# A fused two-block kernel: one more buffer for the experts' weights, and four pieces of side work moved

## What is computed

```
for i in (0, 1):                                   # first block
    mix = gla_mixer(h) if i == 0 else mlstm_mixer(h)
    h = layer_norm(ALPHA * h + mix)
    h = layer_norm(ALPHA * h + grouped_moe(h))     # 16 experts, 2 per token
for l in (0, 1):                                   # second block
    parts = split((rms(x) * (1 + sc1) + sh1) @ w_in[l])
    y_a, y_b = gqa_attention(rope(q), rope(k), v), dilated_attention(...)
    x = x + gt1 * ((gate_a * y_a + gate_b * y_b) @ w_out[l])
    x = x + gt2 * (square(relu(h2 @ w_ff1[l])) @ w_ff2[l])

def grouped_moe(x):
    for e in range(16):
        h = silu(t @ w1[e]) * (t @ w3[e])
        y = y + gates[:, e:e + 1] * (h @ w2[e])
```

## Time and profile before

| what | value |
| --- | --- |
| median of 3 runs | 1483.88 us (1482.96 to 1484.76) |
| profiled execution, its own time | 1485.66 us |
| its span, first to last instruction | 1483.8 us |
| PE busy | 1443.6 us, 97% |
| DVE, ACT, POOL busy | 910.2, 626.7, 40.8 us |
| mean granted TensorE clock | 0.993 |
| moved by DMA | 420.17 MB, mean 283 GB/s |

### The profile page before, as it was taken

The page is one execution under the profiler, slowest core; times in us unless marked ns, Lnnn a source line. Parts: engine busy times, 40 slices in busy tenths (PEclk is TensorE's granted clock), DMA queues, the critical chain, the costliest instruction groups (busy, mean ns, idle before and its releaser), DMA issues.

```text
span 1483.8 us, 20474 instructions
## 1 busy us (share of the span) xinstructions
PE 1443.6 (97%) x8383; PEld 1068.5 (72%) x8383; DVE 910.2 (61%) x1549; ACT 626.7 (42%) x1004; POOL 40.8 (3%) x39
## 2 busy tenths in 40 slices
PE   9999999989999999999799999999999999999998
PEld 7885444436888544443578897999988898799997
DVE  4986111118787611111799888997968976775555
ACT  6453211115334321211555655454456566465443
POOL 0000000000000000000210000000002000000000
PEclk9999999999999999999899999999999999999999
DMA  9897999998467899999665463899955533445540
GB/s 379 314 365 301 426 427 426 427 426 329 166 247 297 331 424 427 427 426 426 247 231 184 181 232 142 335 369 352 357 182 187 197 123 125 151 170 193 179 168 29
DMA packets 59062, 420.17 MB, mean 283 GB/s; under 512 B 6657, under 2 KB 6721, under 8 KB 8658
## 3 DMA queue, kind: packets, MB, share of 16 engines
q1 hardware_dynamic: 58322, 417.17, 71.5%
q0 software_dynamic: 640, 1.61, 0.4%
HBM read 417.71 MB, written 1.05 MB: 282 GB/s over the span
## 4 chain that ended last, share of the span: by engine, by line
PE 80%; DVE 11%; DMA 4%; ACT 3%; issue 1%; SPq 0%; DVEq 0%; ACTq 0%
PE ps L869 78%; DVE lo L2111 2%; DMA AR<-in_moe 2%; DMA raw<-in_moe 2%; DVE AR L2104 2%; PE ps L1520 1%; DMA AR<-in_wgu 1%; DVE AR L2101 1%; PE ps L1491 1%; ACT AR L2011 1%; PE ps L1244 1%; DVE TINY L2104 1%; DVE ACC L2104 0%; PE ps L991 0%; PE ps L1001 0%
## 5 line engine op out<-in xcount | busy, mean ns | idle before, releaser
L2111 DVE TENSOR_TENSOR lo<-raw,hi 128x1024 fp32r<-128x1024 f32 x296 | 359.4, 1237 | 97.7 <-ACT hi L1661 97.0
L1661 ACT ACTIVATE hi<-raw 128x1024 fp32r<-128x1024 f32 x296 | 306.2, 1056 | 183.3 <-PE ps L869 178.1
L869 PE MATMUL ps<-T,hi 128*128 128x256 f32 x1792 | 323.8, 283 | 1.4 <-DVE lo L2111 0.6
L869 PE MATMUL ps<-hi,T 128*128 128x512 f32 x896 | 285.8, 396 | 1.0 <-DVE lo L2111 0.6
L869 PEld LDWEIGHTS ps<-T,hi 128*128 128x128 f32 x1792 | 277.1, 189 | 10.0 <-issue 5.1
L869 PE MATMUL ps<-T,lo 128*128 128x256 f32 x896 | 249.2, 280 | 0.0
L869 PEld LDWEIGHTS ps<-hi,T 128*128 128x128 f32 x896 | 169.0, 189 | 38.0 <-DVE lo L2111 2.1
L869 PE MATMUL ps<-lo,T 128*128 128x512 f32 x448 | 172.8, 390 | 0.0
L869 PEld LDWEIGHTS ps<-T,lo 128*128 128x128 f32 x896 | 169.2, 189 | 0.3 <-DVE lo L2111 0.3
L869 PE MATMUL ps<-hi,AF 128*128 128x512 f32 x512 | 163.3, 391 | 0.0
L2104 DVE SCALAR_TENSOR_TENSOR AR<-AR,ps 128x512 f32<-128x512 f32 x52 | 35.4, 684 | 192.0 <-PE ps L869 104.8
(11 more groups left out here) (247 smaller groups left out, 1730.5 us busy)
## 6 DMA issues: line engine op xcount, KB each, us to landing
raw<-in_moe SPq DMA_DIRECT2D x76, 1024.0 KB, 17.1
raw<-in_b_ff SPq DMA_DIRECT2D x64, 1024.0 KB, 5.3
AR<-in_moe SPq DMA_DIRECT2D x59, 1024.0 KB, 17.1
raw<-in_ada SPq DMA_DIRECT2D x48, 1024.0 KB, 6.7
ring<-in_moe SPq DMA_DIRECT2D x45, 1024.0 KB, 15.8
raw<-in_b_in SPq DMA_DIRECT2D x24, 1024.0 KB, 6.0
raw<-in_b_gate SPq DMA_DIRECT2D x16, 1024.0 KB, 4.8
ACC<-in_moe SPq DMA_DIRECT2D x12, 1024.0 KB, 20.2
```

Source lines behind the costliest of these rows:

```text
L869: return e.matmul(o, l, r, start=a, stop=z, skip_group_check=True)
L1661: e.activation(hi[n % NC][:, :], raw[place[c]][:, 1024 * half:1024 * half + 1024], ACT.Copy).then_inc(*to("hi", "hi", n))
L2111: tt(lo[n % NC][:, :], r, hi[n % NC][:, :], SUB).then_inc(*to("lo", "lo", n))
```

## The change

It has four parts. (1) The second half of TF becomes place 19 (number 13 in `spare`) and takes one chunk in each expert stage, number 11, ahead of the ring, which begins one chunk later; ACC too. In block 0 the arena's buffer AR[2048:4096] (number 6) takes its first chunk two places later. (2) The gathers of group 1, which write the same memory, are moved from pair 0 (steps 2, 3) and pair 1 (steps 1, 4) to pair 1 (two after step 2, two after step 4). (3) In the mLSTM the pace (0, 1, 2, 3, ...) becomes (0, 0, 3, 3, ...). (4) Segment 0's `qk_turn` comes one unit later in both attention layers.

```diff
-            for k, at in enumerate((1, 4) if p else (2, 3)):
+            for k, at in enumerate((2, 2, 4, 4) if p == 1 else (1, 4) if p else ()):
                 if s == at:
-                    yield ("gather", p // 2 + 1, 2 * (p % 2) + k)
+                    yield ("gather", p // 2 + 1, k if p == 1 else 2 * (p % 2) + k)
...
-    pace = iter((0, 1, 2) + 13 * (3,))
+    pace = iter((0, 0) + 14 * (3,))
...
-        turns.append([LAG, n])
+        turns.append([LAG + (n == 0), n])
...
-        raw += [x[:, :] for x in ring] + [ar(0, 2048)]
+        raw += [x[:, :] for x in ring] + [ar(0, 2048), TF[:, 2048:4096]]
...
-                    elif 6 < q < 12:
+                    elif 6 < q < 12 or q == 13:
                         w.wait_ge(*after(*ring_free(i)))
...
-            early = (((4, 0, 95), (5, 1, 76), (3, 5, 5), (1, 6, 95), (2, 7, 95), (6, 19, 95)) if i == 0 else
+            early = (((4, 0, 95), (5, 1, 76), (3, 5, 5), (1, 6, 95), (2, 7, 95), (6, 21, 95)) if i == 0 else
                      ((12, -2, 95), (6, -1, 95), (1, 5, 95), (2, 7, 95), (5, 10, 76)))
-            ring = tuple((7 + n, 11 + n, 80) for n in range(5))
-            spare[i] = [(p, at + c, at + last) for p, c, last in (*early, *ring, (0, 16, 95))]
+            ring = ((13, 11, 11), *((7 + n, 12 + n, 80) for n in range(5)))
+            spare[i] = [(p, at + c, at + last) for p, c, last in (*early, *ring, (0, 17, 95))]
```

## The result

| | before | changed |
| --- | --- | --- |
| median, 17 runs each, on the same chip | 1484.93 us | 1488.32 us |
| lowest to highest | 1482.96 to 1487.16 us | 1485.78 to 1489.04 us |
| ratio, 95% interval | | 1.002 (1.0013 to 1.0027) |
| profiled execution: span, mean clock | 1483.8 us, 0.993 | 1487.1 us, 0.992 |

The change made the kernel slower by 0.2%, 2 to 4 us. 1480.1 us had been forecast, with a range from 1476.8 to 1483.0 us.

A forecast was written before the change was run, and what follows sets the result against it. PE, busy 97% of the span, was taken as the bound, with only idle gaps to win. From the median 1483.9 us, -3.6 - 2.2 + 4.2 - 1.8 - 0.4 = -3.8 gave 1480.1 us, range 1476.8 to 1483.0.

The forecast's parts named there:

- The stall in the mLSTM: Before the first mLSTM values, PE idles 4.3 us for DVE's multiplication in place of 1.3: 3.0 us lost.
- The clock behind it: After the mLSTM's 4.3 us idle, PE's clock falls to half: 1.2 us lost, bounds 0 and 1.7.
- The rule that the prediction quoted from the Trainium skill: For half clock on PE: penalty is throttled time times (1 - K/N); 3.4 us at half clock would cost 1.7.
- The experts: Expert stages: closing holes in the DMA stream wins 3.6 us in block 0 and 2.2 us in block 1.
- the rival "the experts win less": Expert stages: another hole opens where the next buffer is given back; 2.0 us less won, 1482.1 us; chance 0.15.
- The gathers at nothing: Expert stages: moving four gathers wins nothing alone, and their nearer deadline costs nothing.
- no new wait enters PE's work before pair 2: Expert stages: PE waiting for a gather's evacuation before pair 2 would show the forecast wrong; cost taken as nothing.
- The turn of segment 0: Attention layer 0: one unit ahead of the turn fills PE's 2.65 us wait; 1.8 us won, bounds 0.4 and 2.7.
- Layer 1: Attention layer 1: segment 0's later turn wins 0.4 us, bounds 0 and 1.1.
- The rival that the clock falls at segment 1: Attention layer 0: an idle of 2.3 us lowers the clock, so only 0.4 us is won, 1481.5 us; chance 0.12.
- The sum: Whole kernel: gains in experts and turns against the pace's 4.2 us loss give -3.8 us, so 1480.1 us.
- The case "slower": Expert stages gain nothing, so the mLSTM's 4.2 us decide: +2.0 us, 1485.9 us; rival's chance 0.08, slower overall 0.05.

The follow-up runs named there:

- the pace alone: The kernel before with only the mLSTM pace changed to 0, 0, 3, ...: 1492.19 us, ratio 1.0047 to the kernel before.
- the filler's: The changed kernel plus eight unused 128x256 matmuls on PE in the idle before the first mLSTM values: 1484.30 us, ratio 0.9989 to the kernel before.
- the kernel with the experts' parts alone: The kernel before with the new buffer, later arena load and moved gathers, pace and turns as before: 1481.93 us, ratio 0.9976.
- their own run: The kernel before with only the four gathers of group 1 moved later, no new buffer: 1485.68 us, ratio 1.0005.

## Why the prediction was wrong

**The stall in the mLSTM: right.** 3.0 us lost was forecast; the values start 3.1 us later (445.90 instead of 444.85 us, in a kernel that is 2.1 us ahead there). Its reason, DVE's fixed row of work, stands in the rows above.

**The clock behind it: the step that failed.** "An idle of 4.3 us should fall under the same ... I take 1.2 us, bounds 0 and 1.7." It measured 12.73 - 8.00 = 4.7 us, and 11.4 - 8.0 = 3.4 and 12.0 - 8.0 = 4.0 us in the two other profiles with this idle, the changed kernel's second and the pace alone (first to last values 445.58 to 456.99, and 448.27 to 460.27 us). The length of the half clock had been taken over from one shorter idle, 3.4 us for one of 2.65, with a price from one execution. That price itself was right: in the second profile of the kernel before, without the fall, segment 0's turn to segment 1's takes 768.43 - 756.55 = 11.88 us, for 13.25 with it. Nothing in the rows bound it from above: around 715 us the same profile had a half clock of 13.65 us behind an idle of 6.65. The bounds should have reached to such a length, and to some 5 us of cost. The rule that the prediction quoted from the Trainium skill, "TensorE: Matmul & The Clock Gate", section Terms, fits these rows: half of the 9.6 us at half clock from 445.90 to 455.52 us is 4.8 us, and 4.7 were measured; in the other two profiles half of 6.8 and of 8.1 us is 3.4 and 4.0 us, as measured, and in the filler's half of 3.4 us is 1.7, for 1.8. What had been wrong was the length put into it.

**The experts: the mechanism right, the sizes too large.** 3.6 and 2.2 us were forecast; 2.4 us, the forecast's lower bound, and 0.7 us, under its lower bound of 1.4, were measured from the start of a stage's first group to the end of its last (207.8 to 205.4 and 206.2 to 205.5 us in block 0 and 1; block 0 takes 205.3 to 205.5 us in all eight profiles with the buffer and the later arena load and 207.8 to 207.9 in the six others). The stream did gain what was counted. With the stage's later start taken off, chunk 87 landed 3.5 us sooner in block 0 and, counted the same way in the kernel with the experts' parts alone, 2.1 us sooner in block 1. Then it gave 1.0 and 1.4 us back at one load, chunk 89. In the changed kernel SP issues chunk 88 at 296.27 and chunk 89 at 296.64 us; the view of DMA issues has their median us to landing:

```profile
AR<-in_moe SPq DMA_DIRECT2D x1, 1024.0 KB, 17.4
...
raw<-in_moe SPq DMA_DIRECT2D x1, 1024.0 KB, 20.8
```

They land at 313.7 and 317.4 us, 3.8 us apart where 2.44 is the rule. The kernel before has such a gap too, in both blocks, but at chunk 97, 3.8 us behind chunk 96 in block 0 (landings 336.62 and 340.38 us): that load is the next stage's, and no expert waits for it. All the profiles of kernels with both the buffer and the later arena load have it at chunk 89 in block 0, the others at chunk 97; in block 1 it is at chunk 89 (once 86) with the buffer and at 97 without. What makes it is not shown. The DMA packets suggest one cause. In the 3 us before the late landing a read of instructions runs among them:

```profile
q8 instruction: 1, 0.02, 2.3%
```

That is 0.023 x 16 x 3 us, 1.1 us on one engine. In all 14 profiles, in both blocks, a read of this size (16 KB) begins between the landings on either side of the late gap, 28 of 28. The Trainium skill, "DMA: Bandwidth & Descriptors", section "Why a DMA increments its semaphore by 16 and not by 1", says that a transfer's engines finish independently and that it counts as landed only with the last. So a read on an engine that is already behind could move all later landings by its length, and one on an engine that is ahead could leave them alone; no view here shows which engine it met. Reads of this size come about every 25 us, and most leave no gap. No experiment moved one.

I had also put the rival "the experts win less" down to a hole at the next buffer that is given back. The gain was near the rival's (3.1 us for 3.8), its reason was not.

**The gathers at nothing: right**, by their own run. So was that no new wait enters PE's work before pair 2.

**The turn of segment 0: the place right, the size wrong.** It was to win 1.8 us, of which 1.4 as "the clock does not fall". That took one execution's clock for the kernel's. At equal clock it wins 0.4 to 0.5 us. Layer 1: 0.4 us, as forecast. The rival that the clock falls at segment 1 came true in two of seven profiles, so it too is a matter of the execution.

**The sum, as measured in the profiles:** -2.4 - 0.7 + 3.1 + 4.0 (mean of three) - 0.4 - 0.4 = +3.2 us, against +3 us of the ratio. Forecast: -3.6 - 2.2 + 3.0 + 1.2 - 1.8 - 0.4 = -3.8 us. Of the 7 us between, 2.8 lie in the clock behind the stall, 2.7 in the experts and 1.4 in the turn. The first pair of profiles differs by 3.3 us in span too, but is made up otherwise: -2.4 - 0.7 + 3.1 + 4.7 - 2.0 - 0.4 = +2.3 us, and 1.0 us outside the four parts (0.36 us ahead of block 0's experts, and 0.65 us between the mLSTM's second turn and block 1's experts, 27.84 and 28.49 us), which the changed kernel's second profile doesn't show. The case "slower" had been given 0.05 and tied to experts that gain nothing; it came with experts that gained 3 us.

## What to carry to other kernels

Price a new idle of TensorE by what follows it as well: here each of the three idles of 4.5 us cost more through the clock behind it (3.4 to 4.7 us) than by itself (3.1 us), and the way to see it is a window behind the idle, not the gap. Before a difference in a profile is put into a sum, look whether another execution of the same kernel has it. And where a side chain starts from a matmul and ends at the next stage's first one, measure that length: if it stays the same in all versions (11.57 us here), the start of the chain is all that counts, and work can be moved in front of it only where nothing waits.

## What had not been expected of the hardware

- The same idle has different lengths of half clock behind it in executions of the same kernel: 10.2 and 6.8 us behind 4.55 us; 3.4 us or none behind 2.65 us. An idle of only 1.35 us, at the start of attention layer 1, has 3.4 us behind it in 6 of 14 profiles, though 1.5 to 1.8 us at 312 us has none in 14.
- Eight small matmuls in the idle, 3.5 us of work, were enough to keep most of the clock: 3.0 us less in the profile and 4.6 us in the median, though the wait for DVE stayed.
- A saturated queue of equal loads delivers one in 2.44 us, but once in each stage, behind the 30th, one comes 1.0 to 1.7 us late, and everything behind it too. Whether that costs anything depends on whose load it is.
